# Two layers of routed experts: router from raw rows, other slot and loop order, gather with strided weight loads

## What is computed

```python
def hierarchical_moe(h, w_rg, b_rg, w_re, b_re, w_gate, w_up, w_down):
    # h = rms_norm(x, norm_ffn_g[layer]); 4 groups of 8 experts, 512 tokens
    g_logits = xt @ w_rg + b_rg
    g_idx = argmax(g_logits)                       # one group
    e_logits = xt @ w_re + b_re
    top_val, top_idx = top_k(e_logits of that group, 2)
    gates = softmax(g_logits)[g_idx] * softmax(top_val)
    ...
    # per expert e, over the tokens that chose it:
    hid = silu(xb @ w_gate[e]) * (xb @ w_up[e])    # 1024 -> 512
    y = (hid @ w_down[e]) * gate                   # 512 -> 1024
    # summed into each token's row, and x = x + out
```

## Time and profile before

| | us |
|---|---|
| median of 3 runs | 2635.01 |
| the runs | 2633.63 to 2637.3 |
| the profiled execution | 2635.58 |
| its span, first to last instruction | 2634.4 |

### The profile page before, as it was taken

The page is one execution under the profiler, slowest core; times in us unless marked ns, Lnnn a source line. Parts: engine busy times, 40 slices in busy tenths (PEclk is TensorE's granted clock), DMA queues, the critical chain, the costliest instruction groups (busy, mean ns, idle before and its releaser), DMA issues.

```text
span 2634.4 us, 32823 instructions
## 1 busy us (share of the span) xinstructions
PE 2571.3 (98%) x13284; PEld 1785.8 (68%) x13284; DVE 1155.2 (44%) x2171; ACT 896.2 (34%) x1715; POOL 353.1 (13%) x162
## 2 busy tenths in 40 slices
PE   9999999999999999999999999999999999999999
PEld 7875444444777444444477688888888767888887
DVE  2542223322786223322365433562554544465264
ACT  4431111111483111111164554442345445443233
POOL 2200000000340000000031011221222001223212
PEclk9999999999999999999999999999999999999999
DMA  6239999999324999999932022222131212123212
GB/s 217 67 121 419 419 419 419 419 420 419 133 96 158 420 419 420 419 418 420 416 112 80 33 65 78 99 96 96 64 116 56 76 49 65 65 96 114 86 64 80
DMA packets 139321, 543.26 MB, mean 206 GB/s; under 512 B 18976, under 2 KB 30624, under 8 KB 90016
## 3 DMA queue, kind: packets, MB, share of 16 engines
q1 hardware_dynamic: 129264, 536.94, 52.2%
q10 hardware_dynamic: 9904, 4.18, 0.6%
HBM read 538.99 MB, written 2.10 MB: 205 GB/s over the span
## 4 chain that ended last, share of the span: by engine, by line
PE 92%; DVE 5%; ACT 2%; issue 1%; DMA 0%; POOL 0%; SPq 0%; POOLq 0%; DVEq 0%; ACTq 0%
PE ps L618 24%; PE ps L1431 17%; PE ps L620 15%; PE ps L1453 9%; PE ps L1406 5%; PE ps L640 5%; PE ps L552 4%; PE ps L1468 3%; PE ps L1469 2%; PE ps L2035 2%; PE ps L2004 2%; PE ps L553 1%; PE ps L2026 1%; DVE AT L2220 1%; PE ps L470 1%
## 5 line engine op out<-in xcount | busy, mean ns | idle before, releaser
L618 PE MATMUL ps<-w,w 128*128 128x512 f32 x2976 | 679.0, 390 | 2.5 <-POOL w L279 2.5
L618 PEld LDWEIGHTS ps<-w,w 128*128 128x128 f32 x2976 | 557.9, 188 | 119.7 <-POOL w L279 3.4
L279 POOL TENSOR_TENSOR w<-w,w 128x1024 fp32r<-128x1024 f32 (+2 forms) x136 | 329.0, 2427 | 2148.6 <-ACT w L271 2144.3
L1431 PE MATMUL ps<-w,w 128*64 128x512 f32 x2048 | 451.6, 594 | 1.8 <-issue 1.8
L620 PE MATMUL ps<-w,w 128*128 128x512 f32 (+1 forms) x1872 | 408.1, 379 | 3.2 <-DVE w L538 3.0
L271 ACT ACTIVATE w<-w 128x1024 fp32r<-128x1024 f32 (+2 forms) x260 | 252.7, 999 | 415.9 <-PE ps L620 183.6
L620 PEld LDWEIGHTS ps<-w,w 128*128 128x128 f32 x1872 | 337.8, 188 | 69.8 <-issue 4.7
L279 DVE TENSOR_TENSOR w<-w,w 128x1024 fp32r<-128x1024 f32 (+2 forms) x124 | 200.9, 1626 | 385.3 <-ACT w L271 382.8
L1431 PEld LDWEIGHTS ps<-w,w 128*64 128x64 f32 x2048 | 146.0, 137 | 285.5 <-issue 285.5
L1692 DVE TENSOR_TENSOR X<-ps,X 128x512 f32<-128x512 f32 x256 | 162.3, 682 | 181.7 <-PE ps L1469 180.8
L1453 PE MATMUL ps<-w,w 128*64 128x512 f32 x1024 | 226.8, 595 | 0.8 <-ACT w L1520 0.8
(11 more groups left out here) (255 smaller groups left out, 2288.0 us busy)
## 6 DMA issues: line engine op xcount, KB each, us to landing
w<-in_moe_w_gate SPq DMA_DIRECT2D x128, 1024.0 KB, 16.6
w<-in_moe_w_up SPq DMA_DIRECT2D x128, 1024.0 KB, 19.0
w<-in_moe_w_down SPq DMA_DIRECT2D x128, 1024.0 KB, 16.0
w<-in_w_up SPq DMA_DIRECT2D x40, 1024.0 KB, 5.2
w<-in_w_down SPq DMA_DIRECT2D x20, 1024.0 KB, 5.1
w<-in_w_in SPq DMA_DIRECT2D x16, 1024.0 KB, 5.2
w<-in_ab_w_in SPq DMA_DIRECT2D x10, 1024.0 KB, 7.5
w<-in_c_w_in SPq DMA_DIRECT2D x8, 1024.0 KB, 6.9
```

What stands on the lines that cost most here:

```text
L279: up(self.wlo[self.low[s][0]], lane.e.tensor_tensor(lo, raw, hi.bitcast(F32), ALU.subtract))
L618: ins = pe.matmul(bank[:, :], wp[:, k, P * o:P * o + P], ap(k0 + k), start=first, stop=stop)
L1431: ins = pe.matmul(bank[64 * e:64 * e + 64, :], XG[p % 3][:, 4 * u + k, 64 * e:64 * e + 64], w[e][:, k, :], start=(u == 0 and k == 0), stop ...
```

## The change

Six things are different.

1. **Slot order.** The ring of each expert layer starts with slots of the dense ring and of the work space, and ends with the split slots. The dense ring that follows starts at slot 0.
2. **Router from raw rows.** X itself is turned, not HF: 24 transposes ahead of the last chunk of the out product, 4 amid it, 4 behind it. The gain is multiplied into the router's weights once (8 x 64 words), the factor of the row is applied to the logits. The router's weights come packed, in one transfer. The router runs over chunks 0 and 1, then 2, then 3.
3. **Gather rows.** HF is gone. ScalarE and VectorE write the high and low parts of X times the row's factor in the order of x; the block of features 8p + k is then read as the stationary operand with every eighth column (features_of). The gain of the feature is applied when the gathered banks are copied out.
4. **First gather.** All high parts first, then all low parts, over four banks.
5. **first_max** has four operations (a scan that counts the equal ones takes the place of two), and the selection numbers start from 1, so that a subtraction goes.
6. **Loop order.** g and u stand together, combines 0 and 1 behind them, the hidden tile's transposes ahead of combine 2; VectorE's hidden tile stands ahead of its additions.

```diff
-EXPERT_RING = (4, 5, 6, 7, 8, 9, 10, 11, 12, 0, 1, 2, 3)
+EXPERT_RINGS = ((12, 10, 11, 0, 1, 2, 3, 5, 6, 7, 8, 9, 4), (0, 1, 2, 3, 10, 11, 12, 5, 6, 7, 8, 9, 4))
+NRING = len(SLOTS)
 PAIRS = NE // 2
...
+        self.n_dense = 0
         self.ring_start = len(self.halves)
...
+                    if o == outs[-1] and amid and 2 * n_row == len(rows):
+                        amid()
                     for pi, (wp, ap) in enumerate(((hi, a[0]), (hi, a[1]), (lo, a[0]))):
                         ins = pe.matmul(bank_of(o)[:, 0:width], ap(k)[:, P * o:P * o + P], wp, start=(k == 0 and pi == 0),
                                         stop=(hi is rows[-1][0] and pi == 2))
...
+    def features_of(part, c, k):
+
+        return rows_part(part, c).rearrange("t (p i) -> t p i", i=KD)[:, :, k]
...
+    def x_added(lane, layer, c, n):
+
+        lane.wait_total(bx.free, mark["x", layer] + NT * n + c + 1)
+
+    def tensor_turn_rows(layer, kind, c, k0, nk):
+
+        x_added(PE, layer, c, k0 // (KD // 2))
+        bank = banks.take(kind)
+        for j in range(nk):
+            k = k0 + j
+            i = pe.transpose(bank[:, P * j:P * j + P], X[:, c, P * k:P * k + P], ident)
+        up(kind.full, i)
+        mark["turned", layer, c, k0] = (kind, len(kind.banks))
+
...
+    def tensor_turns_ahead(layer):
+
+        mark["x", layer] = len(bx.banks) - 2 * NT + 1
+        for c, kind in ((0, ba), (1, bv)):
+            for k0 in (0, 4):
+                tensor_turn_rows(layer, kind, c, k0, 4)
+        for c, kind in ((2, ba), (3, bv)):
+            tensor_turn_rows(layer, kind, c, 0, 4)
+
+    def tensor_turns_amid(layer):
+        tensor_turn_rows(layer, ba, 2, 4, 4)
+
...
+    def scalar_hi_rows(layer, c):
+        S.wait_total(row_scale, NT * layer + c + 1)
+        up(hb, act.activation(rows_part(0, c), X[:, c, :], ACT.Identity, scale=SM[:, c:c + 1]))
+
+    def vector_lo_rows(layer, c):
+        V.wait_total(hb, NT * layer + c + 1)
+        up(h_row, dve.scalar_tensor_tensor(rows_part(1, c), X[:, c, :], SM[:, c:c + 1], f32(rows_part(0, c)),
+                                           ALU.mult, ALU.subtract))
+
...
+        def tensor_route():
+            early, middle, last = banks.take(blt), banks.take(blt), banks.take(blt_last)
+            tensor_router(layer, early, (0, 1), range(KD // 2))
+            for k0 in (4, 6):
+                tensor_turn_rows(layer, bv, 3, k0, 2)
+            up(blt.full, tensor_router(layer, early, (0, 1), range(KD // 2, KD)))
+            up(blt.full, tensor_router(layer, middle, (2,), range(KD)))
+            up(blt_last.full, tensor_router(layer, last, (3,), range(KD)))
+            PE.wait_total(blt.free, 2 * layer + 1)
+            tensor_fold((0, 1))
+            PE.wait_total(blt.free, 2 * layer + 2)
+            PE.wait_total(blt_last.free, layer + 1)
+            tensor_fold((2, 3))
+            tensor_busy(20)
             PE.wait_ge(masks, 1)
             PE.wait_ge(cb_ready, 2)
             bank = banks.take(bv)
...
+        def tensor_first_gather():
+
+            PE.wait_ge(pick_r, 2)
+            PE.wait_total(hb, NT * (layer + 1))
+            four = [(banks.take(ch), ch) for u in range(2) for ch in (bga, bgv)]
+            for part in range(2):
+                for j, (bank, ch) in enumerate(four):
+                    for k in range(2):
+                        for c in range(NT):
+                            if part:
+                                PE.wait_total(h_row, NT * layer + c + 1)
+                            i = pe.matmul(bank[:, 256 * k:256 * k + 256], features_of(part, c, 2 * j + k), SELR[:, c, :],
+                                          start=(part == 0 and k == 0 and c == 0),
+                                          stop=(part == 1 and k == 1 and c == NT - 1))
+                    if part:
+                        up(ch.full, i)
+
...
         def tensor_gather(q, u):
             PE.wait_ge(pick_r, 2 * q + 2)
-            PE.wait_ge(h_row, 4)
             for j, ch in enumerate((bga, bgv)):
                 bank = banks.take(ch)
                 for k in range(2):
-                    t = P * (4 * u + 2 * j + k)
                     for part in range(2):
                         for c in range(NT):
-                            i = pe.matmul(bank[:, 256 * k:256 * k + 256], HB[part][:, c, t:t + P], SELR[:, c, :],
+                            i = pe.matmul(bank[:, 256 * k:256 * k + 256], features_of(part, c, 4 * u + 2 * j + k), SELR[:, c, :],
                                           start=(part == 0 and c == 0), stop=(part == 1 and c == NT - 1))
                 up(ch.full, i)
...
         def tensor():
             tensor_route()
             tensor_busy(6)
-            tensor_gather(0, 0)
-            tensor_gather(0, 1)
+            tensor_first_gather()
             for p in range(PAIRS):
                 before, after = p > 0, p % 2 and p + 1 < PAIRS
                 PE.wait_ge(bga.free, 2 * (p // 2) + 2)
                 PE.wait_ge(bgv.free, 2 * (p // 2) + 2)
                 tensor_expand("g", bg, p)
+                tensor_expand("u", bu, p)
                 if before:
                     tensor_combine(p - 1, 0)
-                tensor_expand("u", bu, p)
-                if before:
                     tensor_combine(p - 1, 1)
                 if after:
                     tensor_gather(p // 2 + 1, 0)
+                tensor_hidden(p)
                 if before:
                     tensor_combine(p - 1, 2)
                 if after:
                     tensor_gather(p // 2 + 1, 1)
-                tensor_hidden(p)
                 tensor_slots(p)
                 if before:
                     tensor_combine(p - 1, 3)
...
+        def gathered(q, bank, k0):
+
+
+
+            v = bank[:, :].rearrange("p (k e s) -> p k e s", k=2, e=2)
+            a, b = 2 * q % 3, (2 * q + 1) % 3
+            for j in range(2):
+                if b == a + 1:
+                    yield XGS[:, a:a + 2, k0 + j, :], v[:, j, :, :], GK[:, layer, k0 + j:k0 + j + 1], j == 1
+                else:
+                    yield XG[a][:, k0 + j, :], v[:, j, 0, :], GK[:, layer, k0 + j:k0 + j + 1], False
+                    yield XG[b][:, k0 + j, :], v[:, j, 1, :], GK[:, layer, k0 + j:k0 + j + 1], j == 1
+
         def scalar_gather(q, u):
             bank = bga.next(S)
             if q:
                 S.wait_ge(bu.full, 2 * q - 1)
-            v = bank[:, :].rearrange("p (k s) -> p k s", k=2)
-            k = 4 * u
-            up(ss, act.activation(XG[2 * q % 3][:, k:k + 2, :], v[:, :, 0:P], ACT.Copy))
-            bank_to_free(bga, XG[(2 * q + 1) % 3][:, k:k + 2, :], v[:, :, P:2 * P])
+            for dst, src, gain, last in gathered(q, bank, 4 * u):
+                up(bga.free if last else ss, act.activation(dst, src, ACT.Identity, scale=gain))
...
-        def first_max(dst, src, m, pri, n, tmp, vm):
+        def first_max(dst, src, m, restart, n, tmp, count):
             vstep(dve.tensor_reduce(m, src, AX, ALU.max))
             vstep(dve.tensor_tensor(tmp, src, bc(m, [P, 4, n], 2), ALU.is_equal))
-            vstep(dve.tensor_tensor(tmp, tmp, bc(pri, [P, 4, n], 1), ALU.mult))
-            vstep(dve.tensor_reduce(vm, tmp, AX, ALU.max))
-            vstep(dve.tensor_tensor(dst, tmp, bc(vm, [P, 4, n], 2), ALU.is_equal))
+            vstep(dve.tensor_tensor_scan(flat(count), restart, flat(tmp), 0.0, ALU.mult, ALU.add))
+            vstep(dve.scalar_tensor_tensor(dst, count, 1.0, tmp, ALU.is_equal, ALU.mult))
...
             vector_route()
             for p in range(PAIRS):
+                after = p % 2 and p + 1 < PAIRS
+                vector_hidden(p)
                 if p:
                     vector_combine(0)
-                vector_hidden(p)
-                for u in range(2):
-                    if p:
-                        vector_combine(1 + u)
-                    if p % 2 and p + 1 < PAIRS:
-                        vector_gather(p // 2 + 1, u)
+                    vector_combine(1)
+                if after:
+                    vector_gather(p // 2 + 1, 0)
+                if p:
+                    vector_combine(2)
+                if after:
+                    vector_gather(p // 2 + 1, 1)
                 vector_slots(p)
                 if p:
                     vector_combine(3)
```

More of the change, by code:

```diff
@@ L589, in plan_out, with tensor_product @@
             plan_cols((key, n), w, 512 * n, 512, order)
[L591 removed]
+    def tensor_product(key, outs, width, a, kind, ready=None, feature=False, between=None, tail=0, ahead=None,
+                       amid=None):
         bs = {}
```

287 lines of the change are left out of this document (145 added, 142 removed).

## The result

The changed kernel takes 2739.26 us (median of four runs, 2737.36 to 2739.82) against 2634.91 for the kernel before: a ratio of 1.0392, 95% interval 1.0377 to 1.0408. That is slower by 104.3 us. The forecast said slower with 0.57 and named the place, but the range ended at 2738, 1.3 us short.

What follows compares the result with a forecast made beforehand. TensorE was taken as the bound, with the DMA stream nearly equal. From 2635.0 us, -6.6 (entry), -7.8 (loop order) and +98 (strided weight loads) gave 2719; range on record 2615 to 2738, own range 2675 to 2740.

Steps and rivals of the forecast that it cites:

- The bound: Expert stage: TensorE busy throughout, 59.40 us per two pairs; the DMA stream nearly the same bound at 60.1 us.
- Part 4: Gather matmuls: weight loads of every eighth column take 216 ns instead of 120, +98 us over 1024 matmuls.
- Part 1: Stage entry, last addition to X to first gather: raw-row router and shorter selection save 3.3 us per layer, 6.6 in all.
- the arg-max groups: Router selection at the entry: three groups each lose one of five operations of about 0.19 us, -0.6 us.
- the logits: Router output at the entry: transposing X itself, mostly early, brings it a net 1.9 us sooner.
- Part 2: Expert loop order: u straight behind g saves 0.26 us per pair, 3.9 per layer, 7.8 for two layers.
- The island: Combine matmuls between g and u in each pair; removing this separate block was to save 0.26 us per pair.
- Part 3: Slot order: earlier expert loads give 12 to 17 us of lead; worth nothing alone, without it other gains shrink to 2 us per layer.
- Rival 1: Gather: strided load stays hidden under the moving operand, up to 120 ns; total 2621 or 2624 us; chance 0.32.
- Rival 2: Gather: strided load only partly slower, 130 to 170 ns; total 2631 to 2672 us; chance 0.06.
- Rivals 3 and 4: Stream pins the stages, 2631 us with hidden loads, chance 0.03; or granted clock falls in gathers, 2719 to 2940, chance 0.02.
- Rival 4: Gather: granted clock falls; at half of it each slow load takes 216 ns more, 2719 to 2940 us; chance 0.02.

Runs made afterwards that it cites:

- the version with the old loop order: Changed kernel with gather columns made neighbours again and the previous kernel's loop order, so new router and slot order alone: 2627.74 us, ratio 0.9973.
- the contiguous version: Changed kernel with only the row layout undone, so every gather matmul loads neighbouring columns again: 2622.52 us, ratio 0.9949.
- the first run of blocks: Changed kernel plus 18 blocks of 32 independent matmuls behind layer 0's first gather, varying step and operand widths: 119 ns at step 1, 242 at step 8.

## Why the prediction was right or wrong

**The bound.** Right: TensorE had no slack, and all of the dearer gathers showed in the time (121.7 us for the step alone).

**Part 4, the weight loads.** The mechanism was right, and this is the term that was mis-sized: 216 ns per matmul forecast, 238 measured, 98 us against 121. The step that failed is the choice of 216, and of 224 with 12 more as the upper end, from VectorE's price per word. VectorE pays 1.68 times for its words at this step; the weight load pays 2.29 times its 104 ns. At this step each of its columns lies in a line of its own and pays the line's 1.82 ns, which is near VectorE's 1.75 ns per word, while a neighbouring column costs only 0.81 ns. So the time per word carried over nearly (224), the ratio did not (175), and 216 lay below both the 224 and the truth. The expected forms were otherwise as forecast: blocks of 7.6 us (6.9 named), clock at 1.00, DMA share below 1.

**Part 1, the entry.** -3.3 forecast, -3.6 measured per layer; the version with the old loop order has it alone with the slots, -7.6 us for two layers. The parts came as forecast: the arg-max groups -0.6, what follows them -0.8, and the logits -2.3 where -1.9 was said.

**Part 2, the loop order.** -3.9 per layer forecast, -5.4 measured in the changed kernel. The island that goes away is worth 0.36 us per pair, not 0.26. The pair without a gather shows the missing 0.1: g and u took 6.97 + 7.02 = 13.99 us and take 13.83 now, where the forecast took 0.06 off g and nothing off u. The combines, the hidden tile and the slots took 1.13 + 3.83 = 4.96 and take 4.77 now, which is the forecast's 0.2.

**Part 3, the slots.** Right in kind: the others live on it. That it is worth no time alone was not tried. The first expert load came at 105.8, the next six at 141.7 to 144.4 (145 was said), and 13 units had landed before the first expert matmul. Wrong in size: without it parts 1 and 2 together are worth not 2 us per layer but nothing. The loop order spends most of that lead; what the router alone would give with the old slots no run shows. The forecast had also read the lead at the last w_down; at the last w_up it is smaller, 1.5 us.

**The sum.** 2719 forecast, 2739.3 measured: +23 from part 4, -3.7 from parts 1 and 2, +1.2 from clock levels and the wait for a bank, which no term had. The forecast's own range of 2675 to 2740 held the time; the range on record was cut at 2738 to keep 8 in 10, with more trust in 216 than one instruction of another engine can give.

**The rivals.** Rival 1 (the load stays hidden) is wrong, yet its time, 2621 to 2624 with the end of the stages pinned by the stream, is that of the contiguous version, 2622.5. Its argument, that the reads of TensorE were not at their limit, overlooked that a limit per line shows only when the line changes with each word. Rival 2's 130 to 170 ns do not occur at step 8; step 3 comes near them with 173. Rivals 3 and 4 did not happen: the early loads start early, and the clock stays at 1.00 in the strided gathers. Rival 4's price was wrong too: in the first run of blocks the granted clock is 0.50 at 195.4 to 198.4 us, within the strided gather, and its matmuls keep their 240 ns.

## What to carry to other kernels

Give the stationary fp32 operand neighbouring columns, or at most every second one, and pay for the re-ordering where a row is written once: here one write per row on VectorE and ScalarE replaces a surcharge on 1024 loads. The contiguous version's re-ordering writes take 2.0 us each on VectorE and 1.9 on ScalarE where the changed kernel's take 1.3 and 1.1, and no matmul of the gather waits for them. A gain on TensorE in a stage that the DMA engines nearly fill is worth what lead the loads have at the stage's last pair; look at landing against use there before counting it. When several edits come together, measure them one by one: the kept parts of this change are worth 12.8 us, and one part hid them under 121.

## What was not expected of the hardware

- A strided fp32 weight load costs about 1.82 ns per line of 16 bytes (230 to 242 ns for 128 columns at steps of 4 and 8), is free at step 2 and takes 173 at step 3. The price per line doesn't follow TensorE's clock (step 8: 236 to 241 ns at a granted clock of 0.50 to 0.61); the pace per column does (contiguous 104 and 213 ns, step 3 173 and 213, at 1.00 and 0.50).
- Moving columns add next to nothing to a load at step 8: 236 ns with 64 of them, 245 with 512.
- A moving fp32 operand of 256 columns goes from 119 to between 220 and 239 ns as soon as its runs are shorter than four words, pairs included.
- A bf16 weight load takes 29 ns contiguous and 60 at steps of 8 and 16; a moving bf16 operand at step 8 is the dearest of all, 451 ns for 256 columns.
